# Where the gather slots begin in SBUF: moving both expert layers' row buffers to multiples of 512 bytes

## The reference, cut to what matters

```
def peer_ffn(h, w_q, sub_keys, u, v):          # u, v: 16384 rows of 1024 float32 each
    q = (x @ w_q).reshape(n, 8, 2, 128)
    s = einsum('nhpd,hpkd->nhpk', q, sub_keys)
    sv, si = top_k(s, 16)                      # per half; then the 16 best of the 256 sums
    ...
    act = gelu(einsum('nd,nhkd->nhk', xb, u[eb]))
    return einsum('nhk,nhkd->nd', gb * act, v[eb])
```

## Time and profile before

| | |
|---|---|
| median of three runs | 2636.9 us |
| the profiled execution, and its span | 2635.22 us, 2633.4 us |
| busy, share of the span: PE, DVE, ACT, POOL | 89%, 65%, 44%, 33% |
| DMA, mean over the span | 361 GB/s |
| picks of layer 0 | about 274 us to 1700 us |
| picks of layer 1 | about 1970 us to 2625 us |

### The profile page before, as it was taken

How to read it: one execution, slowest core, us unless ns; L and a number is a source line. 1 busy time by engine, 2 the same in 40 slices (tenths; PEclk the granted TensorE clock), 3 DMA queues, 4 the chain that set the end, 5 groups by cost and what they waited for, 6 DMA issues and landing times. The chain is left out here.

```text
span 2633.4 us, 25240 instructions
## 1 busy us (share of the span) xinstructions
PE 2341.5 (89%) x7572; PEld 1277.6 (49%) x7572; DVE 1720.8 (65%) x4232; ACT 1161.2 (44%) x3151; POOL 873.5 (33%) x802
## 2 busy tenths in 40 slices
PE   7999799999998999898989998789989888888786
PEld 3776445543453434454545544477755343333222
DVE  3745988876667656656666776555547666666665
ACT  1351558853535444444444444401425444444434
POOL 0000343434343434434434444200114433444442
PEclk8999899999999999999999999899989999999999
DMA  8423899999999999999999999686059999999997
GB/s 324 165 89 100 348 418 419 403 420 419 396 418 419 419 419 411 420 418 418 418 419 403 419 418 414 243 343 208 25 193 402 422 421 420 421 421 421 421 421 310
DMA packets 146681, 949.70 MB, mean 361 GB/s; under 512 B 16496, under 2 KB 22128, under 8 KB 44272
## 3 DMA queue, kind: packets, MB, share of 16 engines
q0 software_dynamic: 112608, 834.72, 76.9%
q1 hardware_dynamic: 33936, 113.37, 11.6%
HBM read 946.98 MB, written 1.05 MB: 360 GB/s over the span
## 5 line engine op out<-in xcount | busy, mean ns | idle before, releaser
L1080 PE MATMUL pY<-uv,diag 128*128 128x512 f32 x3072 | 1462.2, 613 | 215.1 <-ACT diag L1142 210.5
L1297 DVE SCALAR_TENSOR_TENSOR uv<-uv,H 128x1024 f32<-128x1024 f32 x768 | 939.9, 1224 | 598.5 <-DMA uv<-uv_dram,idx 594.4
L987 POOL DMA_INDIRECT uv<-uv_dram,idx x768 | 851.6, 1109 | 1345.7 <-PE pY L1080 1145.0
L1080 PEld LDWEIGHTS pY<-uv,diag 128*128 128x128 f32 x3072 | 558.3, 192 | 986.5 <-issue 527.1
L1134 ACT ACTIVATE gelu<-dots 128x1 f32<-128x1 f32 x768 | 155.2, 202 | 927.7 <-DVE uv L1297 925.9
L1142 ACT ACTIVATE diag<-cst,coef 128x128 f32<-128x128 f32 x768 | 308.3, 401 | 72.6 <-ACT coef L1138 1.9
L1138 ACT ACTIVATE coef<-gelu,gate 128x1 f32<-128x1 f32 x768 | 226.3, 295 | 28.1 <-ACT gelu L1134 0.4
L1010 PE MATMUL pqs<-hT,wring 128*128 128x256 f32 x544 | 126.8, 388 | 3.9 <-PEq L71 3.9
L127 PE MATMUL plh<-hT,wring 128*128 128x256 f32 x512 | 118.0, 392 | 11.1 <-DMA wring<-hg_zz_dram 8.1
L1010 PEld LDWEIGHTS pqs<-hT,wring 128*128 128x128 f32 x544 | 106.5, 196 | 33.0 <-issue 19.4
L127 PEld LDWEIGHTS plh<-hT,wring 128*128 128x128 f32 x512 | 100.1, 197 | 26.9 <-DMA wring<-hg_zz_dram 8.9
(11 more groups left out here) (424 smaller groups left out, 2092.0 us busy)
## 6 DMA issues: line engine op xcount, KB each, us to landing
wring<-peer_q_dram SPq DMA_DIRECT2D x36, 512.0 KB
arena<-ada_w_dram POOLq DMA_DIRECT2D x8, 2048.0 KB, 10.3
wring<-w_in_dram SPq DMA_DIRECT2D x24, 512.0 KB
aw<-ada_w_dram POOLq DMA_DIRECT2D x6, 2048.0 KB, 10.3
uv<-uv_dram,idx POOLq DMA_INDIRECT x768
arena<-ada_w_dram SPq DMA_DIRECT2D x12, 1024.0 KB
arena<-hg_zz_dram SPq DMA_DIRECT2D x16, 512.0 KB, 7.8
wring<-hg_zz_dram SPq DMA_DIRECT2D x16, 512.0 KB
```

What stands on the lines that cost most here:

```text
L987: nc.gpsimd.indirect_dma_start(out=uv[:, n % SLOTS, :], out_offset=None, in_=t[f"uv{l}"], in_offset=bass.IndirectOffsetOnAxis(ap=idx[:, s ...
L1080: last = nc.tensor.matmul(pY[:, b, half * 512:(half + 1) * 512], diag[:, n % DIAGS, :], uv[:, n % SLOTS, D + half * 512:D + (half + 1) * 512],
L1297: v.scalar_tensor_tensor(out=uv[:, j, 0:D], in0=uv[:, j, 0:D], scalar=1.0, in1=H2[:, own, :], op0=ALU.mult, op1=ALU.mult, accum_out=dots[: ...
```

## The change

`sb` gets an argument `align`, and `uv` is allocated with `align=512` instead of the 32 that everything else has.

```diff
-        def sb(name, shape, dt=FP32, ctx=whole):
-            return ctx.enter_context(nc.sbuf_tensor(name, shape, dt))
+        def sb(name, shape, dt=FP32, ctx=whole, align=32):
+            return ctx.enter_context(nc.sbuf_tensor(name, shape, dt, align_bytes=align))
...
         H2 = sb(f"H2{l}", [P, blocks, D], ctx=c)
-        uv = sb(f"uv{l}", [P, SLOTS, 2 * D], ctx=c)
+        uv = sb(f"uv{l}", [P, SLOTS, 2 * D], ctx=c, align=512)
```

## The result

The changed kernel takes 2603.15 us (median; 2601.71 to 2603.61), the kernel before beside it 2634.68. The ratio is 0.9878, with an interval of 0.9866 to 0.9891: **1.2% faster, 31.5 us**, where I had forecast 5 and a range down to 2620. The profiled execution took 2603.61 us, its span 2601.8 against 2633.4.

The account below looks back on a forecast made before the run. DMA engines were taken to bound both expert stages. Terms of 5.2 us for layer 0's gathers, 0 for layer 1's and 0 for the operands summed to 5.2 us less: 2636.9 - 5.2, given as 2632 us, range 2620 to 2642.

Parts of the forecast that it names:

- What bounds the kernel: Both expert stages: the 16 DMA engines are never idle there, so these stages last as long as their bytes take.
- a nanosecond for each row is worth 6.1 us: Gathers of both layers: 768 picks with 8 rows for each DMA engine, 6,144 rows, turn time per row into kernel time.
- The 1864 us: Time claimed to scale with a row packet's time: 1248 us of layer 0's gathers and 616 of layer 1's.
- The gathers' destination, layer 0: Layer 0's gathered rows written into SBUF: would go at layer 1's pace, 0.42% faster, 5.2 us less.
- The gathers' destination, layer 1: Layer 1's gathered rows, from 64 bytes past a multiple of 256 to a multiple of 512: no gain taken.
- The rival: Gathers of both layers: every start off a 256- or 512-byte boundary costs; 2629, 2624 or 2616 us; chance 0.21.
- The Trainium skill: Gathered rows: its rule of 256-byte transactions with paid-for unused bytes gave 9.6 us less, 2627 us; set aside.
- The operands that DVE reads and writes: DVE's product L1297 on gathered rows: median 1,225 ns in both layers, so 0 change.
- of PE and ACT: Matmuls at 592 ns and `diag` at 401 ns, the same at both layers' starts: 0 change.
- SyncE's loads: Loads to `wring` and `arena`, which stay, and to `keys` and `held`, which move: nothing.
- Slower at remainder 0: Both layers: rows beginning at remainder 0 are written more slowly, 7.8 us more, 2645 us; chance 0.10.
- no effect: Both layers' gathers: the start of a slot makes no difference, 2637 us; chance 0.27.

## Why the prediction was wrong, point by point

- *What bounds the kernel* was right: the DMA engines, in both expert stages. 5.2 ns x 4,096 rows + 4.1 x 2,048 = 30 us is the price list "a nanosecond for each row is worth 6.1 us" at work, and 31.5 were measured. The 1864 us beside it are 3% short, since they leave out the ends of both stages: 4,096 x 312.4 ns + 2,048 x 311.2 ns is 1917 us. That makes no term larger by more than a few tenths.
- *The gathers' destination, layer 0: 5.2 us less* was the mis-sized term. It measured 23.8. The step it priced, from start 32 to 64, exists with the pace that I gave it (33.70 MB in 80 us), and is worth 3 us in the time. What failed is the sentence that if the start is the cause, "layer 0 goes at layer 1's pace after the change". Layer 1 was itself slowed, by 4.1 ns a row, and was no sample of an aligned stream.
- *The gathers' destination, layer 1: I take nothing*, "because the only two starts that the trace has differ by one small step". It measured 8.1 us. This is the step that failed in both terms: the difference of two slowed streams was used as the size of a cost that both had in common. The difference says nothing of that cost, and my upper bound for the rival, two or three such gaps, had no row behind it either; that made the range end at 2620.
- *The rival* of a cost at every start off a multiple of 256, in both layers, was what happened, with 0.21 for it and a time of 2624 (2616 at its far end). I held against it that both layers' rows touch 33 pieces and still differ. Both are true: the extra piece costs 4 ns, and 1 more where an end has a piece of 32 bytes only. Its sizes were taken from the same gap, so even its far end, 20.8 us, was a third too small.
- *The Trainium skill* (DMA: Bandwidth & Descriptors, How a descriptor splits into AXI transactions) had the 256 bytes right, and I set it aside on the sign of the small gap. Its account of the cost, paid-for beats below the start of a read, is not what sets the time here: a shifted read costs nothing (25.62 against 25.63 MB), a shifted write 4 to 5 ns, about the same at 64 and 192. Whether such beats are spent under cover of the write no run shows. The estimate of 9.6 us by that rule was a third of the measured.
- *The operands that DVE reads and writes*, *of PE and ACT*, *SyncE's loads*: 0 each. For what lies behind `uv` the run with only the neighbours moved shows it (0.9997, to 0.1%); for `uv` itself the medians do: 1,224 and 1,225 ns for L1297, 592 for L1080, 401 for L1142.
- *Slower at remainder 0* and *no effect* fell.

## What to carry to other kernels

In a stage that DMA bounds, let the rows that are written into SBUF cover whole pieces of 256 bytes: 4 to 5 ns for each row on its DMA engine, so 1.3% to 1.7% at 8,192 bytes and 2.6% at 4,096, for a few hundred bytes of padding and no instruction. Look at the number of pieces that a row touches, not at its start alone; a start at a multiple of 512 brings nothing over 256. And when a trace has only slowed samples of a cost, their difference bounds nothing: measure the clean case by itself first, which here takes a stream of 80 us.

## What the runs showed of the hardware that I had not expected

- Writing into SBUF, a row whose bytes are spread over one more 256-byte piece than they need takes 3.3 to 5.3 ns longer on its DMA engine: by plain load at every length from 4,096 to 16,384 bytes, by gather at 8,192; a start 16 bytes off costs 6.3. A row longer by one whole piece costs that piece's bytes and nothing extra (316.1 ns at 8,448 bytes against 306.1). The read side, shifted by 32 or 128 bytes in HBM, costs nothing.
- With nothing beside them, the 16 engines moved 427 to 428 GB/s in rows of 8,192 bytes, 430 in rows of 16,384 and 420 in rows of 4,096.
- Loads of SyncE whose rows touch an extra piece show no cost while they are scattered between aligned gathers (8.4% of the time either way), though 2.4 us were at the edge of what these runs can tell. What of the neighbours in the queue makes the difference was not tried.
